# An expert's gate and up matrices loaded as two pieces of 2 KB per partition instead of one of 4 KB

## The chip, the cores and the metric

The kernel runs on one core of a Trainium2 chip. The metric is the device time of one execution in microseconds (us). Before the change it is 1278.8 us, the median of three executions (1276.46 to 1279.06). The traced execution took 1278.63 us, of which the span from the first instruction to the last is 1276.8 us.

## What is computed

One layer of a streaming encoder: 1024 prompt frames behind 16 meta tokens, and 8 running streams with 16 new frames each. A token mixer (pooling branch and sparse attention) comes first, then a mixture of experts, then a last RMS norm. Everything is float32. The part that the change touches is the mixture of experts:

```python
def hier_moe(h, w_rg, b_rg, w_re, b_re, w_g, w_u, w_d):
    ...                                     # pick 1 of 4 groups, then 2 of its 8 experts per token
    act = jax.nn.silu(jnp.einsum('bnd,edf->bnef', h, w_g)) * jnp.einsum('bnd,edf->bnef', h, w_u)
    out = jnp.einsum('bnef,efd->bnd', act * comb.astype(act.dtype)[..., None], w_d)
    return out.astype(h.dtype)
```

There are 32 experts. Each has a gate matrix (1024 x 128), an up matrix (1024 x 128) and a down matrix (128 x 1024), 512 KB each, so 1.5 MB per expert. 1152 tokens go through the layer (1024 prompt frames and 128 new frames), each through two experts: 2304 rows in all, 72 per expert on average.

## The kernel before

The kernel is written with explicit engines and semaphores; the order on every engine is the order of the code. Its stages are the input projection, the pooling branch, index scores and top-k, attention, the two output projections with the router, the experts, and the last norm. The experts run from about 1042 us to 1232 us of the span.

SyncE (SP) issues all weight loads. `load_gate_up(e)` (L841) issues two transfers, the gate matrix (L843) and the up matrix (L844); `load_down(e)` (L846) issues one for the down matrix (L848). All three land in slot `e % 7` of seven slots and count on the semaphore `ew_in` of that slot. In DRAM, gate and up were laid out on the host so that partition p's part of a matrix is one contiguous row of 4 KB: element k*128+f of the row is the weight of input feature 128*k+p and output f. The host's layout is not part of the measured time. The down matrix's rows are 4 KB by nature.

Seven experts are loaded ahead, while the output projection and the router run. From then on a slot is filled again when it comes free: SP waits for `gu_done`, the end of expert e's gate and up matmuls, and issues gate and up of expert e+7; it waits for `dn_done`, the end of expert e-1's down matmuls, and issues the down matrix of expert e+6. SP issues strictly in this order, and all its loads go through one hardware queue, which the profile calls q1.

GpSimd (POOL) does the row traffic of the experts, through its own queue q0. A gather (`gather`, L2528) brings the 128 listed rows of an expert, 4 KB each, into partitions 0 to 127; it is issued three experts ahead. A scatter (L2533) writes the 128 result rows out. Each list has 128 places. Only the first ones, 72 on average, name a token; the others are out of bounds and move no row.

ScalarE (ACT) makes a rounded copy of each expert's gate and up matrices, two experts ahead of the matmuls (`expert_upper`, L1793 and the line behind it). Before that copy it waits for all three transfers of the expert, `ew_in` at 48 per use of the slot. VectorE (DVE) then takes the rest (L2233), and TensorE (PE) runs three float32 products of gate and up (L1365, L1366, L1369), the transposes of the next expert's rows (L1337), and the down product of the expert before (L1350).

After the last expert, SP reads nine times 1 MB of result rows back from DRAM (L901), and the last norm runs on them. Rows that don't fit into an expert's 128 places would be done in a loop at the end (L2560 on), which loads an expert again through q0; its transfers don't appear in this trace.

Of the kernel before, what the change touches and what calls it, by code (L numbers as in the profile page):

```python
# [28 lines left out]
P = 128  # L29
D = 1024  # L30
KD = D // P
# [22 lines left out]
NE, DE = 32, 128  # L54
# [24 lines left out]
def build(nc, a):  # L79
    ctx = ExitStack()  # L80
    with ctx:
# [3 lines left out]
        def sem(name):  # L85
            return ctx.enter_context(nc.semaphore(name))

        def sems(name, n):
            return [sem(f"{name}{i}") for i in range(n)]
# [185 lines left out]
        def stage(s, kk, w):  # L275
            if 4 <= s < KD:
# [54 lines left out]
        eslot = ([RW[:, 0:3072]] + [RH[:, 3072 * i:3072 * i + 3072] for i in range(3)]  # L331
                 + [RQ[:, 3072 * i:3072 * i + 3072] for i in range(3)])
# [8 lines left out]
        def e_down(s):  # L341
            return eslot[s][:, 2048:3072]
# [101 lines left out]
        IDX_KEYS = [[("ki", 0, tt)] + ([("qi", 0, tt)] if tt >= 2 else []) for tt in TILES["idx"]]  # L444
        ROPED = [key for keys in IDX_KEYS for key in keys]
        ROPED += [(kind, b, tt) for kind, b, _, _ in PIECES if kind in ("k", "q") for tt in TILES[kind]]
        RI = {key: i for i, key in enumerate(ROPED)}
        N_IDX = 18
# [3 lines left out]
        PER = 2  # L452

        RUN_Q = [(kind, b, tt) for kind, b, _, _ in PIECES if kind == "q" for tt in TILES[kind]]
        V_HEAD = 2

# [228 lines left out]
        ew_in = sems("expert_weights_in", NSLOT)  # L685
# [15 lines left out]
        ov_w = sem("over_weights_in")  # L701
# [20 lines left out]
        def _(sp):  # L722
# [117 lines left out]

            def load_gate_up(e):  # L841
                s = e % NSLOT
                sp.dma_start(eslot[s][:, 0:1024], a["wg"][e]).then_inc(ew_in[s], 16)  # L843
                sp.dma_start(eslot[s][:, 1024:2048], a["wu"][e]).then_inc(ew_in[s], 16)  # L844

            def load_down(e):  # L846
                s = e % NSLOT
# [2 lines left out]
            def load_e(e):  # L850
                load_gate_up(e)
                load_down(e)
# [18 lines left out]
            load_e(5)  # L871
            sp.wait_ge(hg_in[0], 16)
            load_gate_up(NSLOT - 1)

            def overflow_table_out():
# [9 lines left out]
            for e in range(NE - NSLOT + 1):  # L885
                if e < NE - NSLOT:
                    sp.wait_ge(gu_done, e + 1)
                    load_gate_up(e + NSLOT)
                if e >= 1:
                    sp.wait_ge(dn_done, e)  # L890
                    load_down(e - 1 + NSLOT)
                if e == 2:
                    overflow_table_out()
# [21 lines left out]
        def _(pe):  # L915
# [140 lines left out]
            for n, (kind, b, _, _) in enumerate(PIECES):  # L1056
                if kind not in ("z", "ga", "gb"):
                    continue
                pe.wait_ge(w_lo_done, W_AT[n + 1])
                for cc in range(2):  # L1060
                    for j, (c0, c1) in enumerate(COL3 if kind == "z" else TOK3):
                        o = 0 if kind == "z" else META
                        three(bank_free(U[kind, b, (cc, j)])[:, 0:c1 - c0],
                              lambda k: w_hi(n)[:, k, cc * P:(cc + 1) * P],
                              lambda k: w_lo(n)[:, k, cc * P:(cc + 1) * P],
                              lambda k: h_hi[:, k, o + c0:o + c1],
                              lambda k: h_lo[:, k, o + c0:o + c1]).then_inc(pj_done, 1)
                if n in AFTER:
                    pool_prod(AFTER[n])
# [1241 lines left out]
        def _(pool):  # L2311
# [215 lines left out]
            def gather(dst, idx, s):  # L2527
                pool.indirect_dma_start(out=dst, out_offset=None, in_=h2_d,  # L2528
                                        in_offset=bass.IndirectOffsetOnAxis(ap=idx, axis=0),
                                        bounds_check=TOK - 1, oob_is_err=False).then_inc(s, 16)  # L2530

            def scatter(src, idx, s):
                pool.indirect_dma_start(out=y_d, out_offset=bass.IndirectOffsetOnAxis(ap=idx, axis=0), in_=src,  # L2533
                                        in_offset=None, bounds_check=2 * TOK - 1, oob_is_err=False).then_inc(s, 16)
# [23 lines left out]
            with pool.If(n_over > 0):  # L2558
                pool.wait_ge(dn_done, NE)
                with pool.Fori(0, n_over) as it:  # L2560
                    code = pool.value_load(over_row[0:1, bass.ds(it, 1)], min_val=0, max_val=NE * OVER_J - 1)
                    ex = pool.snap(code % NE, min_val=0, max_val=NE - 1)
                    row = pool.snap((code // NE) * (P * NE - NE) + code + P * NE, min_val=0, max_val=NE * (TOK - P) + NE - 1)
                    for o, src in ((0, a["wg"]), (1024, a["wu"])):
                        pool.dma_start(eslot[0][:, o:o + 1024], src[bass.ds(ex, 1), :, :].rearrange("o p c -> p (o c)")).then_inc(ov_w, 16)
                    pool.dma_start(e_down(0), a["wd"][bass.ds(ex, 1), :, :].rearrange("o p f -> p (o f)")).then_inc(ov_w, 16)
                    pool.dma_start(heads_o[:, :], list_d[bass.ds(row, P, NE), :],
                                   allow_slow_non_contiguous=True).then_inc(ov_l, 16)

                    pool.wait_ge(ov_g, it + 1)  # L2570
                    tt(pjunk[:, 0:1], mhalf, mhalf, ALU.add).then_inc(ov_c, 1)
                    gather(hg[:, 0, :], gidx_o[:, 0:1], ov_h)
                    pool.wait_ge(y_ready, NE + 1 + it)
                    tt(pjunk[:, 1:2], mhalf, mhalf, ALU.add).then_inc(ov_c, 1)
                    scatter(ysb[:, 0, :], heads_o[:, 0:1], ov_y)
                    pool.wait_ge(ov_y, 16 * it + 16)
                    pool.wait_ge(ov_c, 2 * it + 2)
# [87 lines left out]
```

## Time and profile before

| what | value |
|---|---|
| median of three executions | 1278.8 us |
| the traced execution | 1278.63 us, span 1276.8 us |
| PE busy | 1223.0 us, 96% of the span |
| DVE, ACT, POOL busy | 918.7, 512.2, 440.9 us |
| bytes moved by DMA | 163.84 MB in 79456 packets |
| queue q1 (SP's loads and stores) | 64977 packets, 128.84 MB, 29.8% of 16 engines' span |
| queue q0 (POOL) | 12656 packets, 27.62 MB, 6.5% |

A DMA transfer is cut into packets, one for each contiguous piece, and these are spread over 16 DMA engines. A queue's share is the time that its packets took, over 16 times the length of the stretch. So in any stretch, share times 16 times length, divided by the number of packets, is the mean time of one packet on its engine. A share can come out somewhat over 100%, since the packets that overlap a stretch's edges count by their start.

An engine's idle time costs only where that engine is the one waited for. So the busy shares of the whole span say little here, and the stretches of the experts have to be looked at by themselves.

### The profile page before, as it was taken

How to read it: one execution, taken by the hardware profiler on the slowest of the kernel's cores; microseconds unless marked ns; L12 is line 12 of the kernel's file. 1: busy time of each engine (PE TensorE's matmuls, PEld its weight loads, DVE VectorE, ACT ScalarE, POOL GpSimd, SP SyncE). 2: the span in 40 equal slices, each digit the busy share in tenths (PEclk: the TensorE clock that was granted, in tenths of full speed). 3: DMA queues.
4: the chain of work that ended last, by engine and by line, in shares of the span. 5: the costliest groups of instructions: out<-in, count | busy, mean ns of one | idle time of the engine just before them, and what ended most of it. 6: DMA issues, size and time to landing. Idle time of an engine off the chain costs nothing.

```text
span 1276.8 us, 21392 instructions
## 1 busy us (share of the span) xinstructions
PE 1223.0 (96%) x7563; PEld 1066.7 (84%) x7563; DVE 918.7 (72%) x2179; ACT 512.2 (40%) x1117; POOL 440.9 (35%) x740
## 2 busy tenths in 40 slices
PE   6999999999999999998999999999999979998995
PEld 6999999999999999998777667999788858887752
DVE  5657888888999998884667776332666668886747
ACT  6655223232322112324656564100432247765634
POOL 5803575666774115654000000210011233432320
PEclk9999999999999999999999999999999989999998
DMA  7201332222213221102000131944221469999749
GB/s 270 75 30 53 92 72 80 43 79 42 71 43 124 86 84 53 35 1 94 11 1 17 44 98 55 344 133 164 116 83 49 151 228 340 359 341 338 294 165 374
DMA packets 79456, 163.84 MB, mean 128 GB/s; under 512 B 12417, under 2 KB 48081, under 8 KB 78209
## 3 DMA queue, kind: packets, MB, share of 16 engines
q1 hardware_dynamic: 64977, 128.84, 29.8%
q0 software_dynamic: 12656, 27.62, 6.5%
q10 hardware_dynamic: 1728, 6.10, 1.2%
q8 instruction: 61, 1.00, 0.3%
q14 instruction: 34, 0.28, 0.1%
HBM read 137.86 MB, written 39.21 MB: 139 GB/s over the span
## 4 chain that ended last, share of the span: by engine, by line
PE 82%; DMA 7%; DVE 3%; POOL 2%; ACT 2%; SPq 2%; issue 1%; POOLq 0%; ACTq 0%; DVEq 0%
PE bank L921 12%; PE bank L922 12%; PE bank L923 12%; PE bank L1134 5%; DMA region_h<-in_wd 4%; PE bank L1116 3%; PE bank L1218 3%; PE bank L1212 3%; PE bank L1350 3%; PE bank L1052 2%; PE bank L1229 2%; PE bank L1230 2%; PE bank L1231 2%; DMA region_q<-expert_rows_scratch 2%; PE bank L1214 2%; PE bank L1365 1%
## 5 line engine op out<-in xcount | busy, mean ns | idle before, releaser
L1968 DVE MAX8 small<-region_kv 128x8 f32<-128x272 f32 (+4 forms) x241 | 190.2, 828 | 47.6 <-DVE region_kv L1973 47.5
L921 PE MATMUL bank<-h_hi,w_hi 128*128 128x384 f32 (+1 forms) x576 | 196.1, 340 | 0.0
L922 PE MATMUL bank<-h_lo,w_hi 128*128 128x384 f32 (+1 forms) x576 | 196.0, 340 | 0.0
L1973 DVE MATCH_REPLACE8 region_kv<-small,region_kv 128x272 f32<-128x272 f32 (+4 forms) x241 | 195.5, 819 | 0.0
L923 PE MATMUL bank<-h_hi,w_lo 128*128 128x384 f32 (+1 forms) x576 | 194.4, 338 | 0.0
L921 PE MATMUL bank<-w_hi,h_hi 128*128 128x256 f32 x448 | 128.8, 288 | 1.0 <-ACT region_q L1518 1.0
L2331 POOL TENSOR_TENSOR w_lo<-w_stage,w_hi 128x512 fp32r<-128x512 f32 x64 | 80.8, 1293 | 140.6 <-ACT w_hi L1457 140.5
L923 PE MATMUL bank<-w_hi,h_lo 128*128 128x256 f32 x448 | 125.9, 281 | 0.0
L922 PE MATMUL bank<-w_lo,h_hi 128*128 128x256 f32 x448 | 125.9, 281 | 0.0
L923 PEld LDWEIGHTS bank<-h_hi,w_lo 128*128 128x128 f32 x576 | 108.7, 189 | 0.0
L922 PEld LDWEIGHTS bank<-h_lo,w_hi 128*128 128x128 f32 x576 | 108.2, 188 | 0.6
L921 PEld LDWEIGHTS bank<-h_hi,w_hi 128*128 128x128 f32 x576 | 108.0, 187 | 0.5
L1616 ACT ACTIVATE region_q<-bank 128x384 f32<-128x384 f32 x48 | 23.6, 492 | 158.1 <-PE bank L923 158.1
L921 PEld LDWEIGHTS bank<-w_hi,h_hi 128*128 128x128 f32 x448 | 84.2, 188 | 1.7 <-ACT region_q L1518 1.2
L923 PEld LDWEIGHTS bank<-w_hi,h_lo 128*128 128x128 f32 x448 | 84.4, 188 | 0.0
L922 PEld LDWEIGHTS bank<-w_lo,h_hi 128*128 128x128 f32 x448 | 84.3, 188 | 0.0
L2533 POOL DMA_INDIRECT expert_rows_scratch<-region_t,small_i x32 | 39.0, 1218 | 110.4 <-ACT region_t L1808 95.1
L1134 PE MATMUL bank<-region_t,region_kv 128*128 128x512 f32 (+1 forms) x144 | 72.6, 594 | 0.1
L1218 PE MATMUL bank<-o_hi,wao_lo 128*128 128x384 f32 x192 | 67.9, 354 | 0.0
L1365 PE MATMUL bank<-expert_high,rowsT_hi 128*128 128x256 f32 x256 | 65.1, 292 | 1.5 <-ACT rowsT_hi L1801 1.5
L1212 PE MATMUL bank<-o_hi,wao_hi 128*128 128x384 f32 x192 | 65.0, 339 | 0.0
L2102 DVE TENSOR_TENSOR region_t<-bank,region_t 128x384 f32<-128x384 f32 x24 | 13.4, 557 | 70.3 <-PE bank L1218 55.2
(350 smaller groups left out, 3061.2 us busy)
## 6 DMA issues: line engine op xcount, KB each, us to landing
w_stage<-in_w_in SPq DMA_DIRECT2D x72, 256.0 KB, 3.2
region_kv<-in_xa SPq DMA_DIRECT2D x16, 512.0 KB, 6.1
region_h<-in_wg SPq DMA_DIRECT2D x15, 512.0 KB
region_h<-in_wu SPq DMA_DIRECT2D x15, 512.0 KB
region_h<-in_wd SPq DMA_DIRECT2D x15, 512.0 KB
region_q<-in_wd SPq DMA_DIRECT2D x12, 512.0 KB
region_q<-in_wg SPq DMA_DIRECT2D x12, 512.0 KB
region_q<-in_wu SPq DMA_DIRECT2D x12, 512.0 KB
```

The lines of the kernel that those rows point to most:

```text
L921: mm(out, st_hi(k), mv_hi(k), start=(k == 0), stop=False)
L922: mm(out, st_hi(k), mv_lo(k), start=False, stop=False)
L923: last = mm(out, st_lo(k), mv_hi(k), start=False, stop=(k == KD - 1))
L1116: last = nc.tensor.transpose(bank[3 + t % 2][0:rows, r * P:(r + 1) * P], probs_of(x, r)[:, k0:k0 + rows], ident)
L1134: mm(out[:, :], values[0:rows, :], PT[0:rows, t % 3, :], start=(j == 0), stop=False, skip_group_check=True)
L1212: mm(out, hi, o_hi[:, k, c0:c1], start=(k == 0), stop=False, skip_group_check=True)
L1218: last = mm(out, lo, o_hi[:, k, c0:c1], start=False, stop=(k == KD - 1), skip_group_check=True)
L1365: mm(out, rowsT_hi[:, par, k, :], high[:, :, k, :], start=(k == 0), stop=False, skip_group_check=True)
L1968: nc.vector.max(m8[:, q, :], x).then_inc(dve_c, 1)
L1973: nc.vector.match_replace(x, m8[:, q, :], x, TAKEN).then_inc(dve_c, 1)
L2331: tt(w_lo(n)[:, kk * m:kk * (m + 1), :], stage(s if s < KD else s % 4, kk, wd), w_hi(n)[:, kk * m:kk * (m + 1), :].bitcast(F32), ALU.subtr ...
L2533: pool.indirect_dma_start(out=y_d, out_offset=bass.IndirectOffsetOnAxis(ap=idx, axis=0), in_=src, in_offset=None, bounds_check=2 * TOK - 1 ...
```

## The change

In DRAM the gate and up matrices are laid out as (expert, 2, 128, 512) instead of (expert, 128, 1024). Partition p's row of 4 KB becomes two rows of 2 KB, which lie 256 KB apart: the first holds input features of blocks 0 to 3, the second those of blocks 4 to 7. The load's two access patterns become 128 x 2 x 512. What stands in SBUF afterwards is the same as before, element by element. The load in the overflow loop is changed in the same way.

```diff
             def load_gate_up(e):
                 s = e % NSLOT
-                sp.dma_start(eslot[s][:, 0:1024], a["wg"][e]).then_inc(ew_in[s], 16)
-                sp.dma_start(eslot[s][:, 1024:2048], a["wu"][e]).then_inc(ew_in[s], 16)
+                for o, src in ((0, a["wg"]), (1024, a["wu"])):
+                    sp.dma_start(eslot[s][:, o:o + 1024].rearrange("p (n c) -> p n c", n=2),
+                                 src[e].rearrange("n p c -> p n c")).then_inc(ew_in[s], 16)
...
                     for o, src in ((0, a["wg"]), (1024, a["wu"])):
-                        pool.dma_start(eslot[0][:, o:o + 1024], src[bass.ds(ex, 1), :, :].rearrange("o p c -> p (o c)")).then_inc(ov_w, 16)
+                        pool.dma_start(eslot[0][:, o:o + 1024].rearrange("p (n c) -> p n c", n=2),
+                                       src[bass.ds(ex, 1), :, :, :].rearrange("o n p c -> p (o n) c")).then_inc(ov_w, 16)
...
-        "wg": f["w_expert_gate"][0].reshape(NE, KD, P, DE).transpose(0, 2, 1, 3).reshape(NE, P, D),
-        "wu": f["w_expert_up"][0].reshape(NE, KD, P, DE).transpose(0, 2, 1, 3).reshape(NE, P, D),
+        "wg": f["w_expert_gate"][0].reshape(NE, 2, KD // 2, P, DE).transpose(0, 1, 3, 2, 4).reshape(NE, 2, P, D // 2),
+        "wu": f["w_expert_up"][0].reshape(NE, 2, KD // 2, P, DE).transpose(0, 1, 3, 2, 4).reshape(NE, 2, P, D // 2),
```

No instruction is added, taken away or moved. On SP, in the middle of the experts, the loads stand before as follows (region_q, region_h and region_w are the memory of the slots; in_wg, in_wu and in_wd are gate, up and down in DRAM):

```order
L843 DMA region_q<-in_wg 128x1024
L844 DMA region_q<-in_wu 128x1024
L848 DMA region_q<-in_wd 128x1024
L843 DMA region_w<-in_wg 128x1024
L844 DMA region_w<-in_wu 128x1024
```

And at the same place now, where one added line of code moves the line numbers behind it by one and the loop puts gate and up on one line:

```order
L844 DMA region_q<-in_wg 128x2x512
L844 DMA region_q<-in_wu 128x2x512
L849 DMA region_q<-in_wd 128x1024
L844 DMA region_w<-in_wg 128x2x512
L844 DMA region_w<-in_wu 128x2x512
```

The order is the same; the gate and up loads have two pieces per partition, the down load still has one.

## Rows read from the trace of the kernel before

**Rows 1.** The page's 40 slices of the span: DMA busy tenths.

```profile
DMA  7201332222213221102000131944221469999749
```

**Rows 2.** The chain of waits, 1050 to 1135 us: start us, length us, what.

```profile
1056.60 0.96 PE bank L1369 x8
...
1129.05 0.96 PE bank L1369 x8
```

**Rows 3.** The chain of waits from 1135 us on.

```profile
1152.06 23.66 DMA region_h<-in_wd
...
1182.78 6.36 DMA region_t<-ffn_input_scratch,small_i
1189.13 23.82 DMA region_h<-in_wd
...
1242.50 22.29 DMA region_q<-expert_rows_scratch
```

**Rows 4.** Timeline of ACT: start us, length us, instruction, idle before it and releaser.

```profile
1131.45 1.06 ACT L1793 CAST expert_high<-region_h 128x1024 fp32r<-128x1024 f32 x1
1137.80 1.05 ACT L1793 CAST expert_high<-region_q 128x1024 fp32r<-128x1024 f32 x1 [0.66 <-DMA region_q<-in_wd]
...
1215.04 1.05 ACT L1793 CAST expert_high<-region_h 128x1024 fp32r<-128x1024 f32 x1 [2.40 <-issue]
1218.77 1.09 ACT L1793 CAST expert_high<-region_h 128x1024 fp32r<-128x1024 f32 x1
```

**Rows 5.** Busy time by stretch: PE, PEld, DVE, ACT, POOL, PEclk, DMA share, GB/s.

```profile
1047.00:1138.00 91.00, 90.33 (x602) 74.05 (x601) 74.46 (x99) 64.93 (x115) 37.71 (x31) 1.00 0.95 346
1138.00:1200.00 62.00, 57.72 (x370) 45.66 (x369) 43.09 (x58) 38.36 (x70) 18.15 (x18) 1.00 0.92 335
1200.00:1212.00 12.00, 11.64 (x75) 9.06 (x74) 8.62 (x12) 7.54 (x14) 4.04 (x4) 1.00 0.60 228
```

**Rows 6.** DMA queues from 1200 to 1212 us: packets, MB, share of 16 engines.

```profile
q1 hardware_dynamic: 406, 1.48, 30.3%
q0 software_dynamic: 566, 1.24, 28.5%
```

**Rows 7.** The same from 871.5 to 874 us (gated_pool_scratch in rows of 512 bytes).

```profile
q1 hardware_dynamic: 562, 0.29, 39.1%
```

**Rows 8.** The same from 806 to 812 us (in_w_out, rows of 4 KB).

```profile
DMA packets 613, 2.45 MB, mean 409 GB/s; under 512 B 11, under 2 KB 18, under 8 KB 613
q1 hardware_dynamic: 613, 2.45, 102.4%
```

**Rows 9.** The same from 1241 to 1250 us (rows of 8 KB read back).

```profile
DMA packets 529, 3.82 MB, mean 424 GB/s; under 512 B 63, under 2 KB 63, under 8 KB 63
q1 hardware_dynamic: 529, 3.82, 100.7%
```

**Rows 10.** The same from 293 to 300 us (in_w_in, rows of 1 KB).

```profile
DMA packets 1089, 1.07 MB, mean 152 GB/s; under 512 B 64, under 2 KB 1088, under 8 KB 1088
q1 hardware_dynamic: 1088, 1.05, 61.4%
```

**Rows 11.** SP's issues from 1124 us: start us, length us, line.

```profile
1124.47 0.67 SPq L843 DMA_DIRECT2D region_w<-in_wg  x1
1125.19 1.66 SPq L844 DMA_DIRECT2D region_w<-in_wu  x1
```

**Rows 12.** Line L736, loads of w_in: duration ns min/median/max.

```profile
L736 SPq DMA_DIRECT2D w_stage<-in_w_in x76: 367/368/1217, 1.8 to 516.8; - x76
```

**Rows 13.** Waits, 1135 to 1240 us: engine line, releaser, us, times, longest.

```profile
ACT expert_high L1793 <- DMA region_q<-in_wd: 10.9, 5, 2.7
PE bank L1337 <- DMA region_t<-ffn_input_scratch,small_i: 2.1, 2, 1.7
PEld bank L1337 <- DMA region_t<-ffn_input_scratch,small_i: 3.2, 5, 1.9
```

## The prediction, made before the change was run

> **What bounds the kernel now.** I read the page's slices first, to see where DMA is busy at all. For most of the span it is not: the tenths stay at 0 to 3, and they reach 9 only in the slices of the experts and in the last one [rows 1]. A change of DMA packets can count only there. Then I followed the chain of waits through the experts. Up to 1135 us it is TensorE alone: the same group of eight matmuls comes at 1056.60 and at 1129.05 us, 13 experts apart, so one expert takes 72.45 / 13 = 5.57 us [rows 2]. From 1152 us on the chain is made of weight loads: two links of 23.66 and 23.82 us that end with a landing of a down matrix, the second at 1189.13 + 23.82 = 1212.95 us [rows 3]. Behind that come the last matmuls, the last scatter, and 22.29 us in which results are read back.
>
> ScalarE's timeline says what this does to the pace. Its copy of an expert's weights first waits for a landing at 1137.80 us. From there to 1215.04 us there are 12 steps from expert to expert, 77.24 / 12 = 6.44 us each instead of 5.57 [rows 4]. So the weights are late from expert 18 on (the two copies behind 1208.76 us belong to experts 30 and 31).
>
> **When the loads fell behind.** The pace of the loads is not set in the last third alone. Seven slots let the queue fall behind unnoticed. The DMA share is already 0.95 from 1047 us, when expert 7 is asked for, to 1138 us, and 0.92 after it, with the TensorE clock at 1.00 in both [rows 5]. If a queue has work all the time from 1047 us on, every nanosecond added to its work comes out at its end.
>
> I take the engines as unequally loaded. From 1200 to 1212 us the awaited down matrix has not landed, and yet the share is 0.60, with 30.3% for weights and 28.5% for POOL's rows [rows 5, 6]: about 9.4 of 16 engines still work and the others are done. The code offers a cause. Gathers and scatters move only the first 72 rows on average of 128. If eight engines serve the lower 64 partitions, each of them has 24 weight packets per expert (3 matrices x 128 rows / 16), 8 of the gather and 8 of the scatter, 40 packets. At the price of a 4 KB packet below (164 ns) that is 6.56 us, close to the 6.44 us seen. Spread evenly it would be (384 + 144) / 16 = 33 packets, 5.41 us, which TensorE's 5.57 us would cover. So the even spread does not explain a late load, and the uneven one does. In the first phase, POOL's rows come at TensorE's pace: weights for one expert then take W = 3.94 + 2.62 x W / 5.57, so W = 7.4 us, against 5.57 needed. That is why the lag grows from expert 7 on, and why I count from there.
>
> **What the change adds.** Each gate or up matrix goes from 128 packets to 256, so an engine gets 8 more for each, 16 more per expert. The bytes stay the same. What counts is the fixed part of a packet, since two packets of 2 KB differ from one of 4 KB by just that.
>
> The rows give packet prices. 512 bytes: 0.391 x 16 x 2.5 us / 562 = 27.8 ns [rows 7]. 4 KB: 1.024 x 16 x 6 us = 98.3 us for 613 packets, of which 18 are small ones of under 0.4 us together, so 98 us / 595 = 164 ns [rows 8]. 8 KB: 1.007 x 16 x 9 us / (529 - 63) = 311 ns [rows 9]. A straight line through 512 bytes and 4 KB has a slope of 38.9 ns per KB and starts at 8.3 ns. It puts 8 KB at 320, a little over what is seen. I take 9 ns for the fixed part.
>
> Bounds: the line through 4 and 8 KB starts at 164 - 147 = 17 ns. The dearest reading is from 1 KB rows under light load, 0.614 x 16 x 7 us / 1088 = 63 ns with the start of every transfer in it [rows 10]; between 63 and 164, 2 KB would be 97, and a pair 29 ns over one of 4 KB. From below, nothing: a DMA engine that already waits between packets could take the extra one for free. A gain from the packet itself I exclude, since no row shows smaller pieces cheaper per byte.
>
> The sum: 16 packets x 9 ns = 0.144 us per expert, x 24 experts (7 to 30, the last one whose landing is on the chain [rows 3]) = 3.5 us. Bounds 0 and 16 x 29 ns x 24 = 11 us. Expert 31 lands behind expert 30, and its copy starts at 1218.77 us without a wait [rows 4], so it adds nothing.
>
> Edits that I price at nothing. Experts 0 to 6 are loaded while TensorE does the output projection; their 0.144 us each have tens of us of cover. SP's issue: a load with two pieces per partition takes 368 ns to issue at the median [rows 12], where one with 4 KB rows takes about 330; SP waits for slots most of the time, and from 1124 us on its issues are stretched to 0.67, 1.66 and more [rows 11] because the queue has no room. That room will be used up sooner, if it is counted in packets, and SP will stand longer at each issue. Behind it on SP there are only more weight loads, and the engines keep a filled queue meanwhile. If that cover were gone, it would be a gap per transfer, in the dear bound above. The overflow loop isn't run. The last stage reads its 8 KB rows as before.
>
> So 1278.63 + 3.5 = 1282.1 us for the traced execution. That one lies 0.2 us under the median of 1278.8, so I forecast 1282.3 for the time.
>
> **A rule that would make it less.** The Trainium skill, page "DMA: Bandwidth & Descriptors", section "Why small descriptors are slow (HBM only)", gives about 3 cycles of fixed overhead per packet beside one cycle for each 32 bytes. The rows here show 8.3 to 17 ns [rows 7 to 9], which is more. An estimate by that page: a 4 KB packet is 128 such steps in 164 ns, so 3 cycles are 3.8 ns, and the sum would be 24 x 16 x 3.8 ns = 1.5 us, 1280.3 us. It is the second case below.
>
> **Rivals.**
> 1. No measurable change (a change under 0.2%, 2.6 us, can't be told from none here): the fixed part is smaller than 9 ns when packets are queued behind each other, or the engines that set the pace have gaps that take it. At 4 ns the sum is 24 x 16 x 4 ns = 1.5 us, 1280.3. For it: the share is 0.92 to 0.95 and not 1, and the 9 ns are a difference of two rows from stages with other traffic. Against it: the pace of 6.44 us is met by 40 packets without gaps.
> 2. The dear packet: each transfer's start or a lack of prepared packets costs more with 256 pieces, 29 ns per pair, 11 us, 1290. For it: the 1 KB rows [rows 10]. Against it: those transfers are short and far apart, and what one pays at the start is paid once per transfer, the number of which stays.
> 3. Faster: where both queues have work, an engine takes turns between them. With weights in halves, a gathered row waits behind 2 KB and not behind 4. TensorE waits 2.1 us for gathers, its weight loads 3.2 us [rows 13], and one gather of 6.36 us is a link of the chain [rows 3]. If gathers land sooner and this decides, up to the 5.3 us of waits go and 3.5 come, about -2; if the fixed part is hidden as well, -5, so 1274 to 1277. It decides if the last links are gathers rather than weights. Against it: the chain's long links are weights, and on an engine with a full queue the turns change who is first, not when all is done. The same page, section "Queues, rings and completion order", says that an engine goes round its queues packet by packet, many pieces to a packet; no row shows how long a turn is here.
> 4. The change doesn't do what it says, because pieces are cut finer or joined in the hardware before and after alike. Rows of 4 KB appear as packets of about 4 KB (2.45 MB in 613 [rows 8]) and those of 8 KB as packets of 8 KB (3.82 MB in 466 [rows 9]), so I give it no time of its own; it would be 1278.8 and counts with rival 1.
>
> **How the numbers follow.** The forecast (a loss of about 2.6 to 6 us): 0.48. Rival 2 and what lies between: 0.12. Rivals 1 and 4: 0.28. Rival 3: 0.12. That makes slower 0.60, same 0.28, faster 0.12. The likeliest case alone ranges from 1281.4 to 1285. The range for the time goes from 1277, which leaves out most of rival 3, to 1288, which leaves out the end of rival 2.
>
> **What would show it.** The packets of the whole span rise by 64 x 128 = 8192, and q1's share in the experts by the fixed part. The steps of ScalarE's copy go from 6.44 to about 6.58 us. The copy first waits one expert earlier, for expert 17 at about 1134 us, since the first phase's W goes up by 0.144 / (1 - 2.62 / 5.57) = 0.27 us per expert and ten of these are 2.7 us. Expert 30's landing moves from 1213 to about 1216.5, and everything behind it by the same. The stages before 1040 us stay where they are. It is wrong if the steps stay at 6.44 (rival 1), if they go over 6.8 (rival 2), or if the chain of the last 80 us has no weight landing in it any more (rival 3).

## The result, and the profile after

The change made the kernel slower by 2.0 us: 1280.35 us (20 executions, 1277.58 to 1282.14) against 1277.94 us (20 executions, 1275.85 to 1280.37), a ratio of 1.0016 with a 95% interval of 1.0010 to 1.0022. Differences in this document are worked out from such ratios; the two medians lie 2.4 us apart. A second set of times, taken in another session, gave 1.0030 (1.0020 to 1.0040), 3.8 us. The forecast was 3.5 us. The sign holds. The size lies between the two sets: outside the interval of the first (1.3 to 2.8 us) and inside that of the second (2.6 to 5.1 us).

The page of the changed kernel has the two rows that count its packets:

```profile
DMA packets 87648, 163.84 MB, mean 128 GB/s; under 512 B 12417, under 2 KB 48081, under 8 KB 86401
q1 hardware_dynamic: 73169, 128.84, 30.2%
```

There are 8192 packets more, 64 transfers times 128 rows, and not a byte more. Queue q1 was at 29.8% of 16 engines. The 0.4% between are 0.004 x 16 x 1276.8 = 82 us of engine time, 10 ns for each extra packet. The share is rounded to 0.1%, so this is 7.5 to 12.5 ns; it fits the 9 ns of the forecast. The single packet records say the same: the usual duration is 159 ns for a packet of 4 KB before the change and 84 ns for one of 2 KB after it, so a pair has 9 ns more. Whether the path pays these 9 ns is another question, and the answer, further down, is no.

The traced execution after the change has the same span as the one before, 1276.8 us, so their end times can't be compared directly. They can be compared from a common point: the load of expert 7 was issued at 1047.22 us before and at 1046.10 us now. ScalarE's copies of the expert weights now [rows 4]:

```profile
1130.93 1.05 ACT L1794 CAST expert_high<-region_h 128x1024 fp32r<-128x1024 f32 x1 [0.50 <-DMA region_h<-in_wd]
...
1138.80 1.05 ACT L1794 CAST expert_high<-region_q 128x1024 fp32r<-128x1024 f32 x1 [2.79 <-DMA region_q<-in_wd]
...
1215.46 1.05 ACT L1794 CAST expert_high<-region_h 128x1024 fp32r<-128x1024 f32 x1 [2.01 <-DMA region_h<-in_wd]
```

The first wait is for expert 17 now, one expert earlier than before, as forecast (at 1130.93 us, not at 1134). This sign says little, for in the trace of a kernel without the change (the one with a fourth buffer, below) the first wait is for expert 17 too. The copy for expert 30 starts 169.36 us after the load of expert 7, against 167.82 before: 1.5 us later. In between, from expert 18 to 30, the steps are 76.66 / 12 = 6.39 us. They were to rise from 6.44 to 6.58 and did not. "It is wrong if the steps stay at 6.44 (rival 1)", said the prediction, so by this sign of its own rival 1 is the one that came. The section on why the prediction was right says how much the sign is worth.

The same stretches as in [rows 5]:

```profile
1047.00:1138.00 91.00, 90.33 (x602) 74.19 (x602) 74.93 (x98) 64.19 (x113) 37.25 (x31) 1.00 0.95 333
1138.00:1200.00 62.00, 57.50 (x362) 44.59 (x362) 42.66 (x58) 38.80 (x70) 18.59 (x19) 1.00 0.95 339
1200.00:1212.00 12.00, 10.43 (x72) 8.55 (x71) 7.27 (x11) 6.31 (x11) 3.67 (x4) 1.00 0.73 271
```

In the first, the DMA share is still 0.95, but 333 GB/s come of it instead of 346. By their records the engines were as busy and moved 4% less, as a fixed part of each packet would have it. In the second the share rises from 0.92 to 0.95, and the rate from 335 to 339. The TensorE clock stayed at 1.00.

And two rows of TensorE's waits, 1047 to 1245 us, that answer to the last two of [rows 13] (before, these two have the same values in this longer stretch):

```profile
PE bank L1338 <- DMA region_t<-ffn_input_scratch,small_i: 0.6, 2, 0.4
PEld bank L1338 <- DMA region_t<-ffn_input_scratch,small_i: 1.0, 2, 0.6
```

The gathered rows do come sooner: 2.1 and 3.2 us of waiting have become 0.6 and 1.0, and 0.8 and 1.4 in the second trace of the changed kernel. This is what rival 3 expected of turns between the queues. Whether it is worth anything is a question for an experiment.

SP's issues begin to be stretched much earlier than before, where it was at 1124 us [rows 11]:

```profile
1092.49 2.32 SPq L849 DMA_DIRECT2D region_w<-in_wd  x1
```

So the room in the queue looks as if it were counted in packets, or nearly so: it fills when fewer bytes wait in it. Two traces of the experiments below agree. With pieces of 1 KB the first issue of over 2 us comes at 1076 us, and with rows of 8 KB no issue of a weight load takes over 1.1 us, though in that kernel the gathers hold everything up and not the weights.

### The profile page after: what moved, and what is told of

The parts are those of the page before. It is cut to its first block, busy times and chain, and to the rows that moved or that the text cites. A ratio compares the mean times of both kernels' runs of the same rounds, so it can differ in the third digit from the quotient of the medians.

```text
span 1276.8 us, 21392 instructions
## 1 busy us (share of the span) xinstructions
PE 1221.9 (96%) x7563; PEld 1065.6 (83%) x7563; DVE 918.5 (72%) x2179; ACT 512.6 (40%) x1117; POOL 441.3 (35%) x740
## 4 chain that ended last, share of the span: by engine, by line
PE 81%; DMA 6%; SPq 3%; DVE 3%; POOL 2%; ACT 2%; issue 1%; POOLq 0%; ACTq 0%; DVEq 0%
PE bank L922 12%; PE bank L923 12%; PE bank L924 12%; PE bank L1135 5%; PE bank L1219 3%; PE bank L1117 3%; PE bank L1213 3%; PE bank L1351 2%; PE bank L1053 2%; PE bank L1230 2%; PE bank L1231 2%; PE bank L1232 2%; SPq L844 2%; DMA region_q<-expert_rows_scratch 2%; PE bank L1215 2%; DMA region_q<-in_wd 2%
```

## The experiments

Two explanations of the missing part of the 3.5 us were open: a packet costs less than 9 ns on the path (about 5), or it costs 9 ns and something gives a part back, for which the sooner gathers were the candidate. Besides, the forecast stood on three assumptions that no row had shown alone: that engines are loaded unevenly, that what is added from expert 7 on counts, and that the cost grows with the packets.

The edits use both layouts side by side. Each ratio is against the kernel before, run on the same chip.

### Four pieces for every expert

```diff
-                sp.dma_start(eslot[s][:, 0:1024], a["wg"][e]).then_inc(ew_in[s], 16)
-                sp.dma_start(eslot[s][:, 1024:2048], a["wu"][e]).then_inc(ew_in[s], 16)
+                for o, whole, cut in ((0, "wg", "wgc"), (1024, "wu", "wuc")):
+                    if True:
+                        sp.dma_start(eslot[s][:, o:o + 1024].rearrange("p (n c) -> p n c", n=4),
+                                     a[cut][e].rearrange("n p c -> p n c")).then_inc(ew_in[s], 16)
...
```

The matrices `wgc` and `wuc` are added on the host in the layout of four pieces.

> Gate and up of every expert in four pieces of 1 KB per partition instead of one of 4 KB; nothing else changes. Theory A (each extra packet costs 9 ns on the engines that set the pace, 24 experts count, and about 2 us of the landing's delay are covered by another wait behind the last landing): 48 extra packets x 9 ns x 24 = 10.4 us at expert 30's landing, 8 to 9 us in the time. Theory B (the packet costs only what the time of the change showed, 2.0 us for 16 extra packets, so 5 ns, all of it on the path): three times 2.0, 6 us. Theory C (a start cost that grows as pieces get smaller): over 12 us.

Measured: 1285.22 us, ratio 1.0058 (1.0044 to 1.0072), that is 7.4 us (5.6 to 9.2). It lies between theory A's 8 to 9 and theory B's 6, inside the interval of both. Theory C, a cost that grows as pieces get smaller, is out: three times the extra packets cost two to four times as much. Its page:

```profile
DMA packets 104032, 163.84 MB, mean 128 GB/s; under 512 B 12417, under 2 KB 80849, under 8 KB 102785
q1 hardware_dynamic: 89553, 128.84, 30.6%
```

Engine time of q1: 0.306 x 16 x 1283.0 us (its span) = 6282 us, 194 us more than before, for 24576 packets more: 7.9 ns each (7 to 9 with the rounding of both shares). On the path, 7.4 us for 24 x 48 = 1152 packets of one engine are 6.4 ns each, 4.9 to 8.0 by the interval. That leaves out the 9 ns.

### Gate and up as one transfer with rows of 8 KB

```diff
-                sp.dma_start(eslot[s][:, 0:1024], a["wg"][e]).then_inc(ew_in[s], 16)
-                sp.dma_start(eslot[s][:, 1024:2048], a["wu"][e]).then_inc(ew_in[s], 16)
+                sp.dma_start(eslot[s][:, 0:2048], a["wgu"][e]).then_inc(ew_in[s], 32)
```

Two things change here at once, the length of a row and the number of transfers.

> Gate and up of every expert as one transfer with rows of 8 KB, so 8 packets per engine and expert instead of 16. Theory A: 8 packets and one closing packet fewer, 9 x 9 ns x 24 = 1.9 us earlier landing of expert 30, and little or nothing of it in the time, since the other wait behind that landing already ends 2 us after it: -0.5 to 0 us, perhaps up to -1.9. Theory B (5 ns, all on the path): -1.1 us. A price per transfer rather than per packet would show as -2 us or more.

Measured: 1294.14 us, ratio 1.0127 (1.0111 to 1.0142), 16.2 us slower. No theory had this. Its chain of waits, 1040 to 1250 us, says at once what happened:

```profile
1075.50 12.10 DMA region_t<-ffn_input_scratch,small_i
...
1094.70 13.22 DMA region_t<-ffn_input_scratch,small_i
...
1115.03 13.30 DMA region_t<-ffn_input_scratch,small_i
```

The links are gathers now, not weights: seven of them from 1075 to 1210 us, 12.10 to 13.95 us each. The waits of TensorE for them, over the experts:

```profile
PE bank L1336 <- DMA region_t<-ffn_input_scratch,small_i: 20.5, 21, 1.7
PEld bank L1336 <- DMA region_t<-ffn_input_scratch,small_i: 24.8, 21, 1.9
```

The reading is that a gathered row of 4 KB which has to wait behind rows of 8 KB comes late: weights and gathers share the engines by turns of a packet's size, so longer weight packets take time away from POOL's rows, and shorter ones give them time. The rows show that the gathers are late; the turns themselves stand in no trace, and one transfer instead of two was not tried with rows of 4 KB. Fewer and longer packets, hardly cheaper per byte, cost 16 us here.

### A fourth buffer for gathered rows, alone and with the change

If the sooner gathers give back a part of the halves' cost, then giving the gathers more lead by other means should take that gain first. A fourth buffer lets POOL gather four experts ahead:

```diff
+        def hg_of(e):
+            return hg[:, e % 4, :] if e % 4 < 3 else RK[:, 9216:10240]
...
-            for e in range(3):
-                gather(hg[:, e, :], gidx[:, e:e + 1], hg_in[e])
+            for e in range(4):
+                gather(hg_of(e), gidx[:, e:e + 1], hg_in[e])
...
-                if e + 3 < NE:
+                if e + 4 < NE:
                     pool.wait_ge(te_done, 2 * (e + 1))
-                    gather(hg[:, e % 3, :], gidx[:, e + 3:e + 4], hg_in[e % 3])
+                    gather(hg_of(e), gidx[:, e + 4:e + 5], hg_in[e % 4])
```

The transposes on TensorE take their rows and their semaphore from the same four places.

> The layout of before, with a fourth buffer for gathered rows (in memory that is free during the experts), so that each gather is issued one expert earlier. Theory A (in the kernel before, the waits of the transposes for gathered rows hold TensorE back besides the weights, and the copy for expert 30 starts 2.0 us behind its landing): the waits of L1337 for gathers go from 2.1 and 3.2 us to under 0.5, the copy for expert 30 starts within 0.4 us of the landing, and the time falls by 1 to 2 us. Rival (those waits lie beside the waits for weights and cost nothing): within 0.5 us of before.

> The kernel with the fourth buffer for gathered rows in the layout of before, once more, for its trace and a second set of times. Its first times were those of before within 0.1%. If the gathers never cost time, its time is again that of before within 1 us, the waits of L1337 for gathers are gone from its trace all the same, and the copy for expert 30 starts no earlier than before, counted from the load of expert 7. If they do cost time, it is 1 to 2 us under before.

Measured: ratio 1.0002 (0.9993 to 1.0010) in the first set and 1.0002 (0.9993 to 1.0011) in the second, 0.3 us. In the trace of the second no wait of the transposes for gathered rows is left, and TensorE gains nothing. The copy for expert 30 starts at 1215.46 us, 168.68 us after the load of expert 7 (1046.78 us), which is not earlier than before (167.82). So the waits for gathers lay beside the waits for weights. That a gather which goes sooner takes its turns from the weights on the same engines would explain it; it is not shown.

The expectations speak of another wait behind the landing for expert 30, because the copy before starts 2.08 us behind the last landing that the profile shows, 1212.95 us. The packet records speak against such a wait. A load of 512 KB is eight packets of 4 KB on each engine. In the trace before, the last eight of the weights, expert 31's, go through from about 1214.7 to 1216.26 us, so the slowest engine ended expert 30's load only just before, and the copy started 0.4 us later, at 1215.04. With the fourth buffer the same eight begin at 1214.9 us, the copy starts 0.6 us later, at 1215.46, and there the profile names the landing as what released it. So the copy waited for its weights in both, and the time to compare is that of the copy.

> The fourth buffer for gathered rows together with the change. Theory A: with the gathers out of the way there is nothing that the halves can give back, so here they cost their full 24 x 16 x 9 ns, 3 to 3.5 us over the kernel with the fourth buffer alone. Rival (a packet of 2 KB costs 5 ns and not 9): 2.0 us over it, as without the fourth buffer.

Measured: ratio 1.0021 (1.0010 to 1.0032), 2.7 us over before and 2.4 us over the fourth buffer alone (1.0021 against 1.0002). Theory A had 3 to 3.5, the rival 2.0; with an interval of 1.4 us to either side this run does not separate them. But the run without the halves had already shown no gain that could be given back: its interval allows 0.9 us of it at most. My explanation of the missing part by the gathers falls.

> The changed kernel itself once more, on the same chip as the two others: 2.0 us over before, within 1 us.

Measured: ratio 1.0030 (1.0020 to 1.0040), 3.8 us, outside what I had written. The two sets of the same kernel differ by more than chance easily makes, and I don't know why; they come from different sessions. By their medians (1280.48 against 1277.7) the second is 2.8 us, against 2.4 for the first. Taken together, with weights by their intervals, the ratios say that the change costs about 2.5 us.

### Four pieces for a part of the experts

Two kernels; the second has `e >= 18` as its condition.

```diff
+                    if 7 <= e < 18:
+                        sp.dma_start(eslot[s][:, o:o + 1024].rearrange("p (n c) -> p n c", n=4),
+                                     a[cut][e].rearrange("n p c -> p n c")).then_inc(ew_in[s], 16)
+                    else:
+                        sp.dma_start(eslot[s][:, o:o + 1024], a[whole][e]).then_inc(ew_in[s], 16)
```

> Four pieces of 1 KB for gate and up of experts 7 to 17 alone, the ones that are loaded before ScalarE's copy ever waits; all others in one piece of 4 KB. Theory A (the queue on the pacing engines has work from expert 7 on, so a delay there comes out at its end): 48 packets x 9 ns x 11 = 4.8 us at expert 30's landing, 2.5 to 4.5 in the time since about 2 us lie before another wait. Rival (only what is added while the weights are waited for counts, the seven slots cover the rest): 0 to 0.5 us.

Measured: 1280.36 us, ratio 1.0020 (1.0011 to 1.0029), 2.6 us. The rival, that the slots cover everything before the first wait, had 0 to 0.5 and is out. What is added to a queue that is already behind comes out at its end tens of us later, when somebody waits.

> Four pieces of 1 KB for gate and up of experts 18 to 31 alone. Theory A: 48 packets x 9 ns x 13 = 5.6 us at expert 30's landing, 3 to 5 in the time, and the waits of the transposes for gathered rows go away (2.1 and 3.2 us before), since they stand in this stretch. Rival (only these experts count): all of the 7.4 us of the kernel with quarters for every expert.

Measured: 1282.19 us, ratio 1.0032 (1.0021 to 1.0044), 4.1 us. The rival had 7.4 us and is out. The waits of the transposes for gathers fell to 0.4 and 0.9 us. The two parts add up to 6.7 us, and all quarters together cost 7.4. Per extra packet of one engine that is 2.6 us / 528 = 4.9 ns (2.7 to 7.0) and 4.1 us / 624 = 6.6 ns (4.3 to 9.0).

All these kernels can be compared by ScalarE's copies: the start of the copy for expert 30, counted from the load of expert 7, and the mean step from the copy for expert 18 to it. Each row is one traced execution.

| kernel | copy for expert 30, us | mean step, us |
|---|---|---|
| before | 167.82 | 6.44 |
| fourth buffer, layout of before | 168.68 | 6.44 |
| the change, first and second trace | 169.36 and 169.63 | 6.39 and 6.45 |
| quarters for experts 7 to 17 | 169.42 | 6.32 |
| quarters for experts 18 to 31 | 172.64 | 6.64 |
| quarters for all | 174.30 | 6.64 |

Kernels that load the late experts in the same way differ by 0.12 us in the step, which is nearly all of the 0.14 us by which the halves were to raise it. Quarters raise it by 0.2 us, where 48 x 9 ns = 0.43 was expected.

### List places spread over the partitions

This tests the uneven engines. The number of the list place that a partition takes comes from a table of constants, so an edit of this table changes which partitions hold the rows that exist:

```diff
-    c[:, K_END:K_END + P] = np.arange(P)
+    place = np.arange(P)
+    row = 64 * (place % 16 // 8) + 4 * (place % 8) + place // 16 % 4 + 32 * (place // 64)
+    c[:, K_END + row] = place
```

> The layout of before, but a list's place i goes to another partition, so that the 72 rows of a list that name a token stand all over the 128 partitions and not in the first 72 (only a table of place numbers changes). Theory of uneven engines: each DMA engine then has about 33 packets per expert, 5.4 us, and none much over 34; the copies of ScalarE come every 5.6 to 5.8 us to the end instead of 6.44, and the time falls by 7 to 11 us. Theory of one shared limit (memory or fabric, not single engines): the steps stay at 6.4 us and the time within 1 us.

Measured: 1268.81 us, ratio 0.9926 (0.9913 to 0.9940), 9.5 us faster than before. Its copies for the experts 29 to 31:

```profile
1197.26 1.06 ACT L1793 CAST expert_high<-region_h 128x1024 fp32r<-128x1024 f32 x1
...
1202.83 1.06 ACT L1793 CAST expert_high<-region_h 128x1024 fp32r<-128x1024 f32 x1
...
1208.40 1.06 ACT L1793 CAST expert_high<-region_h 128x1024 fp32r<-128x1024 f32 x1
```

No wait stands behind them, and the step is 5.57 us, TensorE's own pace [rows 2]. The stretches:

```profile
1047.00:1138.00 91.00, 90.33 (x602) 74.14 (x602) 74.98 (x99) 66.07 (x117) 37.63 (x31) 1.00 0.99 371
1138.00:1200.00 62.00, 62.00 (x415) 50.94 (x414) 51.20 (x67) 44.72 (x79) 27.30 (x22) 1.00 0.92 344
1200.00:1212.00 12.00, 12.00 (x83) 9.99 (x82) 10.03 (x14) 8.02 (x15) 3.96 (x3) 1.00 0.23 75
```

The same 16 engines move 371 GB/s where they moved 346 [rows 5], and from 1200 us on the weights are all there. The limit was not memory or the sum of the engines. It was the part of them that carried POOL's rows; the run doesn't tell an engine from the way into SBUF that it uses. The Trainium skill, page "DMA: Bandwidth & Descriptors", section "The descriptor swizzle", gives the assignment that the table above was made for: partitions 0 to 63 on engines 0 to 7 and the rest on 8 to 15. The run agrees with it, though the trace doesn't name the engine of a packet.

> The same spread of list places together with the change, gate and up in two pieces of 2 KB. Theory A: where the engines are no longer behind TensorE, 16 more packets per expert (0.14 us) are covered, so the time is that of the spread alone within 1 us, against the 2.0 us that the same change costs without the spread. If the cost of a piece lay elsewhere than in the late weights (at each transfer's start, in SP's issue), the 2 us would stand here too.

Measured: 1268.92 us, ratio 0.9929 (0.9916 to 0.9943), 0.1 us from the spread alone by the medians and 0.4 by the ratios. Here the change costs nothing that can be told; five executions of each would hardly show 1 us, and the run with quarters, next, says it more clearly.

> List places spread over all partitions, and gate and up in four pieces. An engine's load per expert is about 33 packets of 4 KB or 5.41 us, plus 48 x 9 ns = 0.43, 5.84 us, a little over TensorE's 5.57. The seven slots can cover 0.27 us x 24 = 6.5 us of it, so within 1 us of the spread alone (1268.8). If the quarters cost the same 7 us here, the price of a piece isn't a matter of the pacing engines' load.

Measured: 1267.93 us, ratio 0.9915 (0.9900 to 0.9931). Quarters that cost 7.4 us without the spread cost nothing with it, though by their records their packets take as much engine time: q1's share is 30.6% of a span of 1267.4 us against the spread's 29.5% of 1266.3 us, 228 us for 24576 packets, 9.3 ns each.

> List places spread, and gate and up as one row of 8 KB per partition. Without the spread the 8 KB rows cost 16 us, with gathers landing after 12 to 14 us. Theory of turns (an engine serves its two queues by turns, one packet each, so 4 KB rows wait behind 8 KB ones, and that matters because 16 of POOL's packets stand on each pacing engine per expert): with 9 of them per engine a gather and a scatter need fewer turns, and the time comes to 1268 to 1274, most of the 16 us being gone. If the 8 KB transfers themselves were slow, the time would stay at 1280 or more.

Measured: 1275.23 us (1270.8 to 1285.45, ten executions), ratio 0.9985 (0.9961 to 1.0008). The spread takes away most of the 16 us, but the kernel stays 6.4 us over the spread alone (7.5 by the ratios), more than I wrote, and its times scatter widely. TensorE still waits for gathers; the traced execution is one of the longer ones, 1281.47 us:

```profile
PEld bank L1336 <- DMA region_t<-ffn_input_scratch,small_i: 12.1, 15, 1.2
PE bank L1336 <- DMA region_t<-ffn_input_scratch,small_i: 9.1, 15, 1.0
```

So with 8 KB packets the gathers cost time even where the engines are evenly loaded.

## Why the prediction was right, and where its size was off

**The bound.** Right. Weights were late from expert 18 on, the queue was behind from expert 7 on (the quarters for experts 7 to 17 alone cost 2.6 us), and the cause was the uneven load of the engines (the spread took 9.5 us off and brought the step to 5.57 us). The even load would have been covered by TensorE, as the prediction worked out, and with it the change costs 0.1 us. One part of the working was off: at the 155 to 156 ns that a 4 KB packet takes from start to start (next paragraph), 40 packets are 6.2 us and not 6.56, against a step of 6.44 us. The pacing engines have slower packets or gaps besides; no row tells which.

**What the change adds.** 8192 packets, as forecast. The fixed part of 9 ns was read off a line through 512 byte and 4 KB packets; the pages of three kernels give 10, 7.9 and 9.3 ns of recorded time, and the usual records (46 ns for 1 KB, 84 for 2 KB, 159 for 4 KB, 309 for 8 KB) give 8 to 9. But the recorded times of two packets that follow each other on an engine overlap. The kernels with spread places show it in a stretch of 100 us with full queues, 1060 to 1160 us, in one, two and four pieces:

```profile
1060.00:1160.00 100.00, 100.00 (x666) 81.90 (x665) 82.34 (x108) 71.73 (x126) 44.07 (x36) 1.00 1.01 387
1060.00:1160.00 100.00, 100.00 (x666) 81.90 (x665) 82.35 (x109) 71.80 (x127) 44.01 (x36) 1.00 1.03 388
1060.00:1160.00 100.00, 100.00 (x665) 81.95 (x665) 82.64 (x108) 71.64 (x127) 44.13 (x36) 1.00 1.06 376
```

The share goes to 1.06 of what 16 engines have. The edges of so long a stretch can't do that, though the text on the profile before gave them as the reason for shares over 100%. With 25897 packets in the last stretch, 0.06 x 16 x 100 us is 3.7 ns of overlap for each, if the engines never stood idle. The packet records say it directly: a packet of 2 KB with the usual 84 ns is followed, in 72% of the cases in the trace after the change, by one that starts exactly 4 ns before its recorded end (chance alone would make about 10%). From start to start a packet of 1 KB takes 42 to 43 ns in this way, one of 2 KB 80, one of 4 KB 155 to 156, and one of 8 KB 306. So two packets of 2 KB cost 4 to 5 ns more than one of 4 KB on an engine with a full queue, about 4.8, and not 9. The prediction's estimate of 3.8 ns was nearer to that than the 9 ns that I preferred; it rests on the 3 cycles per packet of the Trainium skill, page "DMA: Bandwidth & Descriptors", section "Why small descriptors are slow (HBM only)".

**The sum.** This is the mis-sized term. "16 packets x 9 ns = 0.144 us per expert, x 24 experts" took the difference of recorded durations as the time on the path, 3.5 us. At 4.8 ns the same sum is 1.8 us. The times say 2.0 us in the first set, 3.8 in the second, 2.7 with the fourth buffer. For the quarters 4.8 ns make 5.5 us where 10.4 were expected and 7.4 (5.6 to 9.2) measured; for those of the experts 7 to 17 alone 2.5 us (measured 2.6), for those of 18 to 31 alone 3.0 us (measured 4.1, 2.7 to 5.6). So the overlap explains most of what was missing, and counting from expert 7 was right. What the quarters cost beyond it, some 2 us, stays open. The steps after expert 18 can't settle it for the halves: at 4.8 ns they were to rise by 0.08 us, and kernels without any change there differ by 0.12.

**Experts 0 to 6, SP's issue, the last stage.** Priced at nothing. The halves and quarters under the spread bear it out for the first two: 64 loads with two or four pieces each, and no cost that shows. SP did stand longer at its issues, from 1092 us on, and only weight loads were behind it.

**The rivals.** Rival 1 had given a fixed part "smaller than 9 ns when packets are queued behind each other" as one of its reasons, and this is what the records show: 4.8 ns, close to its 4. The first set's 2.0 us lie under its bound of 2.6 us; the second set and both together do not tell it from the likeliest case. Rival 2 (29 ns per pair) is out. Rival 3's gathers did come sooner with shorter weight packets (waits of 3.2 us became 1.0), but this is worth 0.3 us or nothing, as the fourth buffer shows. Its gain of 5.3 us was added up wrongly besides: the 2.1 and the 3.2 us are one idle time of TensorE, seen once by its matmuls and once by its weight loads, so no more than 3.2 us could go. In the other direction the gathers are worth a lot: with 8 KB packets they become the bound and 16.2 us are lost. Rival 4 is out by the packet count.

It was in part luck that the forecast of the time came so near, 1282.3 us against 1280.35: the price per packet was nearly twice what an engine needs.

## What to carry to other kernels

Before pricing a change of DMA piece size, find out which engines pace the transfer; a scatter or gather that uses only the first partitions can load half of them, and a change of a table that spreads its rows was worth 9.5 us here where the piece size was worth 2 to 4. A packet's fixed part is read off rows of two sizes, but from the start of one packet to the start of the next, since recorded durations overlap: a share over 100% in a long stretch gives this away. It counts from where the queue first falls behind, not from the first wait. And a longer piece is not simply the better one: here a second queue with shorter rows, on which the critical path hung, was served later.

## What was not expected of the hardware

One transfer of 1 MB with 8 KB rows instead of two of 512 KB with 4 KB rows made the gathers beside it land after 12.1 to 13.95 us and cost 16.2 us, although it has fewer packets. The queue between SP and the engines seems to have room for a number of packets rather than of bytes: SP was first held up at 1124 us with 4 KB pieces, at 1092 us with 2 KB and at 1076 us with 1 KB pieces. Taking waits for gathers away (2.1 and 3.2 us of them, down to none) changed the time by 0.3 us. And a packet's recorded duration is 3 to 4 ns longer than what its engine spends on it in a full queue, which makes a fixed part of 9 ns out of one of 4.8.
